# Shifted moving operands, mirrored chunks and merged score products in a tuned encoder block

## The chip, the cores and the metric

The kernel runs on one core of one Trainium2 chip. The metric is the device time of one execution in microseconds. Three runs of the kernel before gave 1113.47, 1114.10 and 1114.87 us; the median is 1114.1 us. TensorE (PE) does the matrix products, VectorE (DVE), ScalarE (ACT) and GpSimd (POOL) the rest, SyncE (SP) issues most of the transfers.

## The reference

One layer of a streaming encoder on 512 positions of 1024 columns: half an FFN, a token mixer, cross attention to 256 memory rows, half an FFN, a final norm. All of it is float32.

```python
x = x + 0.5 * swiglu(rmsnorm(x, ffn1_norm), ffn1_w_gu, ffn1_w_down)
x = x + token_mixing(rmsnorm(x, mix_norm), w_in, lower_bounds, hg_norm, conv_w, conv_norm, w_out)
x = x + cross_attention(rmsnorm(x, xa_norm), rmsnorm(mem, mem_norm), xa_wq, xa_wkv, xa_wo)
x = x + 0.5 * swiglu(rmsnorm(x, ffn2_norm), ffn2_w_gu, ffn2_w_down)
return rmsnorm(x, final_norm)
```

The mixer has four recurrent heads, f = lb + (1 - lb) * sigmoid(fz), k = 1 - f, S_t = diag(f_t) S_{t-1} + k_t v_t^T, o_t = S_t^T silu(q_t), each normed and gated by silu(g), beside a short convolution gb * (3 taps over gc * u) on 512 channels.

## The kernel before

**Products.** An exact product is made of three: each operand is split into a high and a low part of a fast type (`wh`, `wl` for weights, `xh`, `xl` and others for activations), and `product` issues high x high, high x low and low x high. The first operand of a matmul is stationary and is loaded into the array, the second moves through it. ACT makes a unit's high part (`hi`), POOL its low part (`lo`, four instructions of 256 columns); a unit is 1024 columns of weights, and four slots of units rotate. In the FFNs 30 column pairs are computed by seven products of half size (`pair`, `seven`): 256 moving columns each. The other groups move 512.

**Where the operands lie.** Worked out from the allocations, modulo 128 columns of 4 bytes: in the 512-column groups stationary and moving operand both start at column 32; in the 256-column products of the pairs the stationary one starts at 112 and the moving one at 32, as in the two halves of the last group of the second FFN. The 256-column products of the memory's keys (`mh`, `wh`) and of the attention scores (`kTh`, `qhl`) have both at 32. The slots of `wh` and `wl` are read in two ways for this, 48 columns apart (`wh_apart`, `for_256`).

**The mixer.** 28 slots (`MIX_SLOTS`) hold one group of 24 products each, of kind f, q, g (a head's gate, query and output gate), v, B, C or u. After its group, a slot runs the steps of `STEPS` on every engine in the same order. A head starts at slot 0, 7, 12 or 17 and takes nine steps in nine slots: A (log of f, running sum `b` within chunks of 128), L0, L1, L2 (two of the seven levels each, the seventh in L2), K, Q, S, O, N. The decay within a chunk is split into levels of block size 64 to 1: at each level DVE makes the differences of `b` to the block's middle (`differences`, L1250 and L1251), ACT takes their exponential (`decays`), DVE multiplies by q and k (`factors`, L1258 and L1259), PE makes the level's scores (L1740, four matmuls, one for each chunk, of the 64 queries that lie in second halves), and DVE copies them through a mask into `attn` (`take_scores`). PE takes the scores of levels 0 and 1 in step L1, 2 and 3 in L2, 4 and 5 in K, level 6 and the diagonal in Q. Q also transposes the decayed keys, S makes the chunk states, O the output, N the sum of squares for its norm. These small products are float32 and not split; the profile writes two records for each such matmul.

**Order.** Each engine's instructions stand in the order in which the code issues them; semaphores alone join the engines. PE starts a group when the unit's low part is ready and the bank of four groups before has been read (`group_read`).

## Time and profile before

| | us |
|---|---|
| median of three runs | 1114.1 |
| the profiled execution | 1113.43 |
| its span in the trace | 1111.6 |
| PE busy, share of the span | 1100.8, 99% |
| DVE / ACT / POOL busy | 633.8 / 527.4 / 437.1 |
| time in which PE waited for another engine, all rows | 3.8 |

Stages by the trace: first FFN 0 to 357 us (its pairs 72 to 216), mixer 352 to 553, output projection and the memory's keys to 622, cross attention to 757, second FFN to the end (its pairs 802 to 966). The granted clock of PE is 0.998 over the span. A busy PE says little on its own here, since a matmul's record runs on while the next one has started; distances between starts say what one costs.

### The profile page before, as it was taken

The numbers are of one execution on the slowest core, as the hardware profiler recorded it, in microseconds if no ns is written. First come the engines' busy times: TensorE is split into PE (matmuls) and PEld (weight loads), VectorE is DVE, ScalarE is ACT, GpSimd is POOL, SyncE is SP. The second block draws the span as 40 slices with busy tenths as digits, with TensorE's granted clock in tenths as the row PEclk, the third lists the DMA queues.
The fourth block names the chain that finished last, engine by engine and source line by source line (L and its number), as shares of the span: only waits on it lengthen the run. The fifth ranks groups of instructions, "written<-read, shape, count | busy, mean of one in ns | idle before, by whom it ended". The sixth has DMA issues, their size and how long they took to land.

```text
span 1111.6 us, 17495 instructions
## 1 busy us (share of the span) xinstructions
PE 1100.8 (99%) x6434; PEld 972.6 (87%) x6434; DVE 633.8 (57%) x923; ACT 527.4 (47%) x735; POOL 437.1 (39%) x545
## 2 busy tenths in 40 slices
PE   9999999999999999999999999999999999999997
PEld 8889999988888888888888888888899999988886
DVE  7887777442222668888668133466977777440012
ACT  6455555542324555654366443354555555542221
POOL 0000000486665544434548883163000000485651
PEclk9999999999999999999999999999999999999999
DMA  7287675332333221222313442122676675332312
GB/s 241 79 229 184 179 198 170 115 112 97 113 100 108 76 77 57 76 76 77 114 57 127 158 170 76 39 77 76 180 199 180 170 196 170 115 114 96 112 57 76
DMA packets 49458, 136.89 MB, mean 123 GB/s; under 512 B 4736, under 2 KB 11008, under 8 KB 49280
## 3 DMA queue, kind: packets, MB, share of 16 engines
q1 hardware_dynamic: 43888, 118.90, 30.7%
q0 software_dynamic: 4320, 15.73, 8.2%
q10 hardware_dynamic: 1200, 1.57, 0.4%
q8 instruction: 34, 0.56, 0.2%
q14 instruction: 16, 0.13, 0.0%
HBM read 134.09 MB, written 2.10 MB: 123 GB/s over the span
## 4 chain that ended last, share of the span: by engine, by line
PE 53%; POOL 25%; issue 21%; DVE 0%; POOLq 0%; ACT 0%; DVEq 0%
POOL wl L465 25%; PE bank L1497 8%; PE bank L1499 8%; PE bank L1498 8%; PE bank L1606 4%; PE bank L1604 4%; PE bank L1605 4%; PE score L1606 3%; PE score L1604 3%; PE score L1605 3%; PE o_bank L1606 1%; PE o_bank L1605 1%; PE o_bank L1604 1%; PE bank L1561 1%; PE bank L1569 0%
## 5 line engine op out<-in xcount | busy, mean ns | idle before, releaser
L465 POOL TENSOR_TENSOR wl<-raw,wh 128x256 fp32r<-128x256 f32 x511 | 410.9, 837 | 324.7 <-ACT wh L507 281.3
L507 ACT ACTIVATE wh<-raw 128x1024 fp32r<-128x1024 f32 (+1 forms) x120 | 125.6, 1052 | 148.1 <-PE bank L1499 144.0
L1497 PE MATMUL bank<-xh,wh 128*128 128x512 f32 x456 | 182.2, 400 | 0.0
L1499 PE MATMUL bank<-xh,wl 128*128 128x512 f32 x456 | 177.8, 390 | 0.0
L1498 PE MATMUL bank<-xl,wh 128*128 128x512 f32 x456 | 177.7, 390 | 0.0
L479 POOL DMA_DIRECT2D raw<-w_all x30 | 26.1, 868 | 324.8 <-DMA raw<-w_all 324.8
L1497 PE MATMUL bank<-zr,wh 128*128 128x512 f32 (+1 forms) x374 | 140.8, 377 | 0.0
L1499 PE MATMUL bank<-zr,wl 128*128 128x512 f32 (+1 forms) x374 | 140.7, 376 | 0.0
L1498 PE MATMUL bank<-zr,wh 128*128 128x512 f32 (+1 forms) x374 | 140.7, 376 | 0.0
L950 DVE SCALAR_TENSOR_TENSOR x<-bank,x 128x512 f32<-128x512 f32 (+1 forms) x31 | 21.3, 686 | 173.0 <-PE bank L1499 173.0
L1498 PEld LDWEIGHTS bank<-xl,wh 128*128 128x128 f32 x456 | 85.7, 188 | 18.7 <-issue 1.7
L1497 PEld LDWEIGHTS bank<-xh,wh 128*128 128x128 f32 x456 | 85.7, 188 | 18.6 <-issue 1.2
L1499 PEld LDWEIGHTS bank<-xh,wl 128*128 128x128 f32 x456 | 85.6, 188 | 18.2
L520 ACT ACTIVATE wh<-raw 128x1024 fp32r<-128x1024 f32 x50 | 52.8, 1057 | 86.6 <-PE bank L1499 54.7
L1014 DVE TENSOR_TENSOR wl<-raw,wh 128x1024 fp32r<-128x1024 f32 x72 | 87.4, 1216 | 1.4 <-ACT wh L520 0.9
L1498 PEld LDWEIGHTS bank<-zr,wh 128*128 128x128 f32 x374 | 70.3, 188 | 12.9
L1499 PEld LDWEIGHTS bank<-zr,wl 128*128 128x128 f32 x374 | 70.2, 188 | 13.0
L1497 PEld LDWEIGHTS bank<-zr,wh 128*128 128x128 f32 x374 | 70.2, 188 | 12.8
L1497 PE MATMUL bank<-cat_h,wh 128*128 128x512 f32 x128 | 50.6, 395 | 0.5 <-POOL wl L465 0.5
L1498 PE MATMUL bank<-cat_l,wh 128*128 128x512 f32 x128 | 49.9, 389 | 0.0
L1499 PE MATMUL bank<-cat_h,wl 128*128 128x512 f32 x128 | 49.8, 389 | 0.0
L930 DVE TENSOR_TENSOR acc<-acc,sq 128x512 f32<-128x512 f32 x43 | 42.7, 992 | 9.5 <-ACT sq L542 6.6
(304 smaller groups left out, 2586.9 us busy)
## 6 DMA issues: line engine op xcount, KB each, us to landing
raw<-w_all SPq DMA_DIRECT2D x200, 512.0 KB, 3.3
raw<-w_all POOLq DMA_DIRECT2D x30, 512.0 KB, 5.2
zf<-w_all SPq DMA_DIRECT2D x30, 256.0 KB, 4.4
x<-x_t SPq DMA_DIRECT2D x8, 256.0 KB, 6.1
out_t<-x SPq DMA_DIRECT2D x8, 256.0 KB, 2.5
raw<-w_all SPq DMA_DIRECT2D x6, 256.0 KB, 6.1
memf<-mem_t ACTq DMA_DIRECT2D x1, 1024.0 KB, 4.7
raw<-w_all ACTq DMA_DIRECT2D x2, 256.0 KB, 3.9
```

What stands on the lines that cost most here:

```text
L465: ins = nc.gpsimd.tensor_tensor(l[:, slot, two], raw[:, slot, two], h[:, slot, two].bitcast(f32), SUB)
L479: pool.dma_start(raw[:, 2 * p + 1, :], w_all[u, :, :], accum_op=ADD).then_inc(up_added[p], 16)
L507: nc.scalar.activation(unit_hi(u)[:, 0:wide], raw[:, slot, 0:wide], ACT.Copy).then_inc(hi_ready, 1)
L520: nc.scalar.activation(unit_hi(u), raw[:, slot, :], ACT.Copy).then_inc(hi_ready, 1)
L930: V_.tensor_tensor(acc[:, :], acc[:, :], sq[:, n % 2, :], ADD).then_inc(sq_added, 1)
L1014: V_.tensor_tensor(unit_lo(u), raw[:, slot, :], unit_hi(u).bitcast(f32), SUB).then_inc(lo_ready, 1)
L1497: nc.tensor.matmul(out_, a[0], b_[0], start=first, stop=False)
L1498: nc.tensor.matmul(out_, a[0], b_[1], start=False, stop=False)
L1499: return nc.tensor.matmul(out_, a[1], b_[0], start=False, stop=last)
L1604: nc.tensor.matmul(out_, a[0][:, ks], bh, start=first and k == 0, stop=False, skip_group_check=True)
L1605: nc.tensor.matmul(out_, a[0][:, ks], bl, start=False, stop=False, skip_group_check=True)
L1606: last = nc.tensor.matmul(out_, a[1][:, ks], bh, start=False, stop=k == 3, skip_group_check=True)
```

## The change

What the code does differently:

1. The weights have one reading again; in its place `xh` and `xl` get a second one 48 columns further (`xh_apart`), and the other moving operands of the pairs are shifted alike. Modulo 128 columns the stationary operands are all at 32 and the pairs' moving ones at 80. The eight 512-column groups of each FFN that use the normed x (`src=made`) read the shifted copy as well, the last group's halves no longer do.
2. In the mixer every second chunk (0 and 2) is stored mirrored in time, q and f in one tile `qf`. Two chunks then make one 128-wide problem: a level takes two matmuls of 128 queries in place of four of 64. Scores gather in `tri`, and one more masked copy (`triangles`) spreads them over `attn`. Reading and writing q, f and the output takes two instructions of 256 columns where it took one of 512; `factors` is one of 512 where it was two of 256.
3. The masks for this are built on the chip: `make_masks` on DVE ahead of the first FFN's down groups, two matmuls with a mirrored identity (`swap`) ahead of slot 0, two DVE additions after it. Two tiles of V are mirrored by matmuls of 512 columns in float32 (`turn_v`) in slot 6.
4. The difference and exponential of the chunk's end (`kd`) move from K to L2, level 6's difference to L1; ACT runs steps L1 and L2 ahead of a unit's high part; the norm of a head runs a slot later; two heads' convolution taps run a slot later; q2, q3 stand earlier. The product of C and rstd is made once, with rstd squared.

```diff
-             ("B", 0), ("q", 2), ("f", 3), ("g", 1), ("C", 1), ("u", 1),
-             ("q", 3), ("g", 2), ("g", 3), ("B", 1), ("C", 2), ("u", 2), ("B", 2), ("C", 3), ("u", 3), ("B", 3)]
+             ("q", 2), ("B", 0), ("f", 3), ("g", 1), ("q", 3), ("C", 1),
+             ("u", 1), ("g", 2), ("g", 3), ("B", 1), ("C", 2), ("u", 2), ("B", 2), ("C", 3), ("u", 3), ("B", 3)]
...
-                            lhs = X[:, x_slot(l), :]
-                            rhs = lhs.rearrange("p (t n s m) -> p t n s m", t=TT, s=2, m=LEVELS[l])[:, :, :, 1, :]
-                            width = 64
...
-                        for t in range(TT):
-                            last = nc.tensor.matmul(score_bank[s % 2][:, width * t:width * (t + 1)],
-                                                    lhs[:, 128 * t:128 * t + 128], rhs[:, t], start=True, stop=True)
+                        if l < len(LEVELS):
+                            for g in range(2):
+                                last = nc.tensor.matmul(sc[:, 128 * g:128 * g + 128], keys_of(l, g), queries_of(l, g),
+                                                        start=True, stop=True)
...
+        def queries_of(a, g):
+            at_, m = XW * x_slot(a) + 256 * g, LEVELS[a]
+            halves = X[:, at_:at_ + 2 * (256 + m)].rearrange("p (s w) -> p s w", s=2)[:, :, 0:128]
+            return halves.rearrange("p s (n z m) -> p n s z m", z=2, m=m)[:, :, :, 0, :]
...
+            def turn_v(t):
+                if t == 0:
+                    pe.wait_ge(group_read, G_V + TT + 4)
+                else:
+                    pe.wait_ge(v_ready, 1)
+                nc.tensor.matmul(o_bank[:, :], swap.bitcast(f32), V[:, t, :], start=True, stop=True).then_inc(v_turned, 1)
...
+            pe.wait_ge(masks_in, 1)
+            nc.tensor.matmul(score_bank[0][:, :], swap, lower[:, 0:512], start=True, stop=True)
+            nc.tensor.matmul(score_bank[1][:, 0:384], swap, lower[:, 512:896], start=True, stop=True).then_inc(masks_out, 1)
...
-                xx, qq, kk = (blocks(t_, m) for t_ in (X[:, x_slot(a), :], qb[:, h % 2, :], fb[:, h % 2, :]))
-                V_.tensor_tensor(xx[:, :, 1, :], xx[:, :, 1, :], qq[:, :, 1, :], MULT)
-                V_.tensor_tensor(xx[:, :, 0, :], xx[:, :, 0, :], kk[:, :, 0, :], MULT).then_inc(score_in, 1)
+                V_.tensor_tensor(level, level, qk, MULT).then_inc(score_in, 1)
...
+                early = [st for st in STEPS[at] if st[0] == "L" and st[2] > 0]
+                for st in early:
+                    step(*st)
                 ahead(U_MIX + at)
...
-                        act.wait_ge(x_old, (KC - 1) * which + 2 * i + 2)
+                        act.wait_ge(x_old, (KC - 1) * which + 2 * i + 3)
...
-                        group(u0 + P_UNIT, g0 + P_UNIT)
+                        group(u0 + P_UNIT, g0 + P_UNIT, src=made)
```

**PE, slot 6 (the group of f1, then step Q of head 0).** Before:

```order
L1499 MATMUL bank<-xh,wl 128x512
L1740 MATMUL score<-X 128x64 x4
L1740 MATMUL score<-qb,fb 128x128 x4
L1751 MATMUL n_bank<-ident,kd 128x128 x4
L1497 MATMUL bank<-xh,wh 128x512
```

Now, with `qf` for q and f and `both` for the decayed keys:

```order
L1631 MATMUL bank<-xh,wl 128x512
L1857 MATMUL o_bank<-V,ubr 128x512
L1873 MATMUL score<-X 128x128 x2
L1877 MATMUL score<-qf 128x128 x4
L1888 MATMUL n_bank<-ident,both 128x128 x4
L1857 MATMUL o_bank<-V,ubr 128x512
L1629 MATMUL bank<-xh,wh 128x512
```

The level's four matmuls have become two twice as wide, and the two mirroring matmuls stand around the step; their second waits for DVE to have copied out the first.

**DVE, around slots 17 and 18, where head 3 starts.** Before, from the running sum of head 3 to its first differences:

```order
L1285 SCALAR_TENSOR_TENSOR b<-restart,ubuf 128x512
L1389 TENSOR_SCALAR ubuf<-convU,par 128x512
L1390 SCALAR_TENSOR_TENSOR ubuf<-convU,par,ubuf 128x512
L1392 SCALAR_TENSOR_TENSOR ubuf<-convU,par,ubuf 128x512
L1394 TENSOR_TENSOR ubuf<-ubuf,rstd 128x512
L1358 SCALAR_TENSOR_TENSOR qb<-bank,rstd 128x512
L1361 SCALAR_TENSOR_TENSOR qb<-gbuf,qb 128x512
L1328 COPY S<-n_bank 128x128
L1330 SCALAR_TENSOR_TENSOR S<-S,eb,n_bank 128x128 x2
L1250 TENSOR_TENSOR X<-b 128x4x64
```

Now:

```order
L1382 SCALAR_TENSOR_TENSOR b<-restart,lf 128x516
L1502 TENSOR_TENSOR convU<-bank,ubuf 128x512
L1422 COPY S<-n_bank 128x128
L1424 SCALAR_TENSOR_TENSOR S<-S,both,n_bank 128x128 x2
L1345 TENSOR_TENSOR X<-b 128x4x64
L1346 TENSOR_TENSOR X<-b 128x4x64
L1345 TENSOR_TENSOR X<-b 128x8x32
L1346 TENSOR_TENSOR X<-b 128x8x32
L1355 TENSOR_TENSOR X<-X,qf 128x4x2x64
```

The four tap instructions and the two of q no longer stand between the running sum and the differences.

**ACT, slot 14 (f3; step O of head 1, step L1 of head 2).** Before, from the sigmoid of f3 to the exponentials:

```order
L796 ACTIVATE fb<-fb 128x512
L507 ACTIVATE wh<-raw 128x1024
L780 ACTIVATE osq<-o_bank 128x512
L759 ACT_TABLE_LOAD
L759 ACTIVATE X<-X 128x512 x2
```

Now:

```order
L852 ACTIVATE qf<-qf 128x2x2x128
L815 ACT_TABLE_LOAD
L815 ACTIVATE X<-X 128x2x16x16
L815 ACTIVATE X<-X 128x2x32x8
L815 ACTIVATE X<-X 128x2x256
L562 ACTIVATE wh<-raw 128x1024
L838 ACTIVATE osq<-o_bank 128x512
```

The square of the output (`osq`), for which PE's step N waits, now stands behind three exponentials and a unit's high part.

## Rows read from the trace of the kernel before

**Rows 1.** three mixer stretches: us, then each engine's busy us (instructions)
```profile
427.00:457.00 30.00, 29.24 (x159) 24.84 (x158) 25.48 (x44) 17.34 (x22) 13.08 (x16) 1.00 0.16 53
457.00:488.00 31.00, 31.00 (x176) 26.59 (x176) 26.01 (x47) 20.89 (x26) 13.30 (x16) 1.00 0.24 85
488.00:520.00 32.00, 31.04 (x169) 26.23 (x168) 28.12 (x52) 14.63 (x21) 12.31 (x15) 1.00 0.15 51
```

**Rows 2.** PE in order of time: start us, us, what, records
```profile
383.38 1.89 PE L1740 MATMUL score<-X 128*128 128x64 f32 x16
385.08 0.48 PE L1497 MATMUL bank<-wh,xh 128*128 128x512 f32 x1
...
397.95 1.00 PE L1740 MATMUL score<-X 128*128 128x64 f32 x8
398.78 1.11 PE L1740 MATMUL score<-qb,fb 128*128 128x128 f32 x8
399.73 0.60 PE L1751 MATMUL n_bank<-ident,kd 128*128 128x128 f32 x4
...
411.82 1.05 PE L1770 MATMUL o_bank<-attn,V 128*128 128x128 f32 x8
412.71 0.83 PE L1775 MATMUL o_bank<-qb,S 128*128 128x128 f32 x6
```

**Rows 3.** groups of instructions: all the level scores | busy us, mean ns
```profile
L1740 PE MATMUL score<-X 128*128 128x64 f32 x224 | 27.1, 272 | 1.7 <-DVE X L1259 1.7
```

**Rows 4.** PE, a float32 product of 512 columns and its followers
```profile
541.25 1.02 PE L1781 MATMUL n_bank<-osq,ones 128*128 128x512 f32 x2
541.70 0.80 PE L1497 MATMUL bank<-xh,wh 128*128 128x512 f32 x1
542.34 0.40 PE L1498 MATMUL bank<-xl,wh 128*128 128x512 f32 x1
```

**Rows 5.** PE starts 48 records apart: pairs, memory keys, last group
```profile
150.08 0.28 PE L1604 MATMUL score<-xh,wh 128*128 128x256 f32 x1
155.73 0.28 PE L1604 MATMUL score<-zr 128*128 128x256 f32 x1
...
598.53 0.28 PE L1499 MATMUL bank<-mh,wl 128*128 128x256 f32 x1
604.29 0.28 PE L1499 MATMUL bank<-mh,wl 128*128 128x256 f32 x1
...
1087.32 0.28 PE L1499 MATMUL bank<-zr,wl 128*128 128x256 f32 x1
1092.97 0.28 PE L1499 MATMUL bank<-zr,wl 128*128 128x256 f32 x1
```

**Rows 6.** DVE, start of the mixer [idle before, releaser]
```profile
360.05 0.69 DVE L1356 TENSOR_TENSOR fb<-bank,rstd 128x512 f32<-128x512 f32 x1 [1.44 <-issue]
...
368.43 0.68 DVE L1358 SCALAR_TENSOR_TENSOR qb<-bank,rstd 128x512 f32<-128x512 f32 x1
```

**Rows 7.** PE at the bank that q0 leaves
```profile
368.70 0.39 PE L1499 MATMUL bank<-wh,xl 128*128 128x512 f32 x1
369.17 0.50 PE L1497 MATMUL bank<-wh,xh 128*128 128x512 f32 x1
```

**Rows 8.** DVE, the factors of one level, slow and fast
```profile
417.64 0.95 DVE L1259 TENSOR_TENSOR X<-X,fb 128x256 f32<-128x256 f32 x1
418.52 0.41 DVE L1258 TENSOR_TENSOR X<-X,qb 128x256 f32<-128x256 f32 x1
```

**Rows 9.** PE where it waited for DVE, heads 1 and 3
```profile
435.20 2.00 PE L1740 MATMUL score<-X 128*128 128x64 f32 x16 [0.76 <-DVE X L1259]
...
497.44 2.00 PE L1740 MATMUL score<-X 128*128 128x64 f32 x16 [0.96 <-DVE X L1259]
```

**Rows 10.** ACT, slot 14
```profile
459.58 1.06 ACT L507 ACTIVATE wh<-raw 128x1024 fp32r<-128x1024 f32 x1
460.54 0.58 ACT L780 ACTIVATE osq<-o_bank 128x512 f32<-128x512 f32 x1
```

More of the change, by code:

```diff
@@ L99 @@
     _s.sort(key=lambda st: st[0] == "N")
+NORMED = [[h for kind, h, _ in (STEPS[at - 1] if at else []) if kind == "N"] for at in range(len(MIX_SLOTS))]
 def block_kernel(nc, w_all, x_t, mem_t, params, consts_mask, ident_d, out):
@@ L461, in _, with lo @@
         def _(pool):
-            def lo(slot, h=wh, l=wl, pieces=KC):
-                for k in range(0, pieces, 2):
+            def lo(slot):
+                for k in range(0, KC, 2):
                     two = slice(128 * k, 128 * k + 256)
-                    ins = nc.gpsimd.tensor_tensor(l[:, slot, two], raw[:, slot, two], h[:, slot, two].bitcast(f32), SUB)
+                    ins = nc.gpsimd.tensor_tensor(wl[:, slot, two], raw[:, slot, two], wh[:, slot, two].bitcast(f32), SUB)
                 ins.then_inc(lo_ready, 1)
@@ L488, in _ @@
             pairs(U_FFN2, 1)
-            whole(U_FFN2 + P_UNIT, NU - SLOTS)
-            for u in range(NU - SLOTS, NU):
-                pool.wait_ge(hi_ready, u + 1)
-                if for_256(u):
-                    lo(u % SLOTS, wh_apart, wl_apart)
-                else:
-                    lo(u % SLOTS, pieces=DOWN_SPLIT[-1])
+            whole(U_FFN2 + P_UNIT, NU)
         @block.scalar
@@ L503, in hi @@
                 act.wait_ge(raw_loaded[slot], u // SLOTS * 16)
-                nearer = for_256(u + 1 - SLOTS) and not for_256(u)
-                wide = 128 * DOWN_SPLIT[-1] if u == NU - SLOTS else UNIT
-                act.wait_ge(unit_used, u + 1 - SLOTS + nearer)
-                nc.scalar.activation(unit_hi(u)[:, 0:wide], raw[:, slot, 0:wide], ACT.Copy).then_inc(hi_ready, 1)
+                act.wait_ge(unit_used, u + 1 - SLOTS)
+                nc.scalar.activation(wh[:, slot, :], raw[:, slot, :], ACT.Copy).then_inc(hi_ready, 1)
             def ahead(u):
@@ new lines, in silu @@
+            def silu(kind, c):
+                dve.wait_ge(act_out, FN[kind, c] + 1)
+                if kind == "g":
+                    dst = gb[:, c % 2, :]
+                    V_.scalar_tensor_tensor(out=dst, in0=half_tanh, scalar=1.0, in1=dst, op0=ADD, op1=MULT)\
+                        .then_inc(silu_done, 1)
+                else:
+                    for p in range(2):
+                        dst = q_of(c)[:, :, p, :]
+                        last = V_.scalar_tensor_tensor(out=dst, in0=by_chunk(half_tanh)[:, :, p, :], scalar=1.0,
+                                                       in1=dst, op0=ADD, op1=MULT)
+                    last.then_inc(silu_done, 1)
@@ new lines, in taps @@
+            def taps(at, c):
+                dve.wait_ge(group_read, SLOT_GROUP[at] + 5)
+                w = [pcol("convw", CC * k + c) for k in range(3)]
+                link(V_.tensor_scalar(convV, convU[:, 2:], w[2], None, MULT))
+                link(V_.scalar_tensor_tensor(out=convV, in0=convU[:, 1:1 + T], scalar=w[1],
+                                             in1=convV, op0=MULT, op1=ADD))
+                link(V_.scalar_tensor_tensor(out=convV, in0=convU[:, 0:T], scalar=w[0],
+                                             in1=convV, op0=MULT, op1=ADD))
+                link(V_.tensor_tensor(convV, convV, rstd[:, :], MULT))
@@ L1595, in ffn @@
                     group(u0 + c, g0 + c, release=x_old if c == 2 * old - 1 else None)
+                made = xh_apart, xl_apart
                 for c in range(2 * old, 2 * pre):
-                    group(u0 + c, g0 + c, ready=(xn_lo, KC * which) if c == 2 * old else None)
+                    group(u0 + c, g0 + c, src=made, ready=(xn_lo, KC * which) if c == 2 * old else None)
                 def seven(out_, a, at, b_, cols_, first):
@@ L1659, in ffn @@
                 for c in range(P_UNIT + 1, N_UP):
-                    group(u0 + c, g0 + c)
+                    group(u0 + c, g0 + c, src=made)
                 ud, gd, nd = u0 + N_UP, g0 + N_UP, len(DOWN_SPLIT)
@@ L1694, in ffn @@
                         for k in range(n):
[L1695 removed]
+                            last = product(bank[(gd + KC - 1 + h) % 4][:, HALVES[h]], wpair(u % SLOTS, 128 * k, 128 * k + 128),
                                            (hid(j)[0][:, HALVES[h]], hid(j)[1][:, HALVES[h]]), j == 0, j == FC - 1)
```

389 lines of the change are left out of this document (245 added, 144 removed).

## The prediction

> **What bounds the kernel now.** I read the busy shares first, then the waits of PE, then PE in order of time. PE is busy for 99% of the span at full clock, and all its waits for other engines come to 3.8 us (both in the table above), of which 1.7 lie in the mixer, at two places [rows 9]. So the time is the sum of the distances between PE's starts, and an edit counts by what it does to that sum or by a wait that it brings. PE cannot run ahead of DVE, though: in the mixer DVE is busy for 25.5 of 30, 26.0 of 31 and 28.1 of 32 us [rows 1], 86% of the stretch. No other stage of the change has an engine that close behind PE.
>
> **Scores of the levels, removed and added.** Before, 224 records of 64 columns [rows 3] stand in what would be 14 blocks of 16. One block takes 385.08 - 383.38 = 1.70 us [rows 2], so 14 take 23.8 us. A matmul is two records: 0.213 us. Now there are 56 matmuls of 128 columns. Rows show two of this size: the attention's 8 records in 0.89 us, 0.111 each, and the diagonal's 8 records in 0.95 us, 0.119 each [rows 2]. I take the middle, 0.115: 112 records are 12.9 us. The term is -10.9 us, with -11.4 and -10.5 as near ends. That a matmul of twice the columns costs nearly the same is the heart of the forecast. What the rows cannot show is the new reading pattern: two runs of queries, at level 1 every second element. At 64 columns the same stride cost nothing (level 6's block of 8 records took 0.83 us [rows 2], half a block and no more), but the stream was then shorter than what bounds the product, and now it is about as long. A float32 product of 512 columns takes 542.34 - 541.25 less 0.23 for the split product between, 0.86 us [rows 4], so a stream of 128 is worth 0.215 us; doubled it would be 0.43. For level 1 alone that is 8 x 0.2 = 1.6 us, for all seven 11 us. I take none of it, since the strides at 64 columns cost nothing, and keep both ends.
>
> The Trainium skill speaks against the gain. Its page "TensorE: Matmul & The Clock Gate", section "Back-to-back issue gap", gives the distance of two matmuls as columns over 2.4 GHz and a small constant, while its section on LDWEIGHTS gives a load as 128 columns over 1.2 GHz, whatever is streamed. By the first the 28 x 64 and 14 x 128 columns of a head cost the same and the term is near zero; by the second it is near a half. The trace agrees with the second: 0.106 and 0.111 us for a record of 64 and of 128 columns [rows 2].
>
> **Mirrored V, added.** Two float32 matmuls of 512 columns on PE's path, 0.86 us each [rows 4]: +1.7 us. The second waits until DVE has copied the first out, about 0.7 us for an instruction of 512 columns from PSUM [rows 6]. Between them stand level 6 (2 matmuls), the diagonal (4) and four transposes, over 1.5 us, so I cost that wait at nothing; without the cover it would be 0.7. DVE has no work due then.
>
> **Masks, added.** The two matmuls ahead of slot 0 move 896 columns of the split type; at 0.118 us for 256 [rows 5] that is +0.4 us. `make_masks`, some 25 DVE instructions of at most 0.7 us, stands ahead of the down groups, where each group gives PE 15 us of work (66 products at the 0.23 us of a split product of 512 columns) and DVE 3 instructions; it is hidden. At the mixer's start DVE gets two additions from PSUM, a memset and rstd squared ahead of f0: 0.69 + 0.5 + 0.3 + 0.7 = 2.2 us (0.69 for 512 columns from PSUM [rows 6], the smaller ones by their columns). DVE sat idle for 1.44 us there [rows 6], so f0 comes 0.8 us later, and with it the running sum of head 0 and the reading of q0 behind it. PE already waits for q0's bank: 369.17 - 368.70 is 0.47 where 0.23 is usual [rows 7]. PE itself comes 0.4 later, so this wait grows by 0.4 us: +0.4. The scores of levels 0 and 1 come after it and gain from the shorter `factors`; no wait there.
>
> **Waits in the mixer.** The two old ones go, -1.7 us [rows 9]. Head 1's came from the norm and the product of C ahead of the differences, head 3's from four taps and q3; all four pieces are moved or gone, as the order shows. Two new kinds are possible. First, slot 19 now holds g2, step L1 of head 3 and the taps: 0.7 + 4 differences + 2 copies + 2 factors of 512 + the two differences of level 6 + 0.7 + 2.7 us. With 0.34 us between the fast instructions of 256 columns this is 8.4 us, and about 10 when POOL works beside it (0.95 against 0.41 us for one instruction [rows 8]). PE's work from that slot to the next is 5.4 us for its group (24 products of 0.227), 1.6 for step Q and 0.9 for step S or K, 7.9 us. DVE starts slot 20 some 2 us late, needs 4 to 6 us to the factors of level 5, and PE needs them 6.9 us after its own group: a wait of about 1 us. Second, ACT's square of the output in slots 14 and 19 now stands behind the exponential of level 6, for which DVE must have done that slot's factors, and a unit's high part: DVE 4.9 to 8.6 us, then 0.6 + 1.06 + 0.58 [rows 10] gives 7.2 to 10.9 us after the group, against 8.8 us until PE's step N. Half a microsecond each, twice. Together +2.0 us; the ends are 0 and 5.
>
> The units' high parts also stand behind L1 and L2 on ACT, and POOL's low parts and PE's group behind them. They are made three slots, about 20 us, before PE needs them; a delay of 9 us is hidden. DVE's extra copy (0.7 us a head) is paid by the product of C that is gone (0.7), the split reads (0.07 each) by the merged factors.
>
> **The shift of the operands.** The distance between stationary and moving operand, modulo 128 columns, is 112 - 32 = 80 in the pairs before and 32 - 80 = -48, again 80, now. The pairs run at 5.65 / 48 = 117.7 ns, and the keys of the memory, distance 0, at 5.76 / 48 = 120.0 ns [rows 5]. Same distance, same cost: the term of 2520 products is 0. Sixteen groups of 512 columns, 384 products, go from distance 0 to 80. No row has 512 columns at 80; by the 2.3 ns of the 256-column rows that is -0.9 us, by the same in the other direction +0.9. I take -0.4, half of the nearest row. The last group's 132 products go from 80 (117.7 ns, rows 5) to 0: +0.3 us. ACT's split of the normed x waits for one more of PE's k steps, 0.7 us, in a stretch where the result is ready more than 1 us early: nothing.
>
> **Sum.** -10.9 + 1.7 + 0.4 + 0.4 - 1.7 + 2.0 - 0.4 + 0.3 = -8.2 us. The profiled execution took 1113.4 us, its span 1111.6, the rest start and end that stay; 1113.4 - 8.2 = 1105.2. It lies 0.7 below the median of the runs, so I forecast 1105.9 us.
>
> **Rivals.**
> 1. DVE becomes the bound of the mixer. For: the 86% of rows 1, and PE's share of a head shrinks by 2.7 us while DVE's work does not. Against: 93 us with 79.6 busy become 86.4 us, so DVE would be at 92%, under 1. If the contention of rows 8 strikes more of the merged 512-column instructions, waits of 7 us rather than 2: 1111. The skill's page "SBUF — State Buffer", section "Who interferes with whom", says that a DVE instruction with two SBUF inputs and a GpSimd instruction that reads SBUF lock each other out entirely; the two times of one instruction in the trace agree with that. It gives no time of its own here.
> 2. The distance counts with its sign, not modulo 128. Then the pairs move by the 2.3 ns of rows 5 or more: 2520 x 2.3 = 5.8 us. Dearer: 1111.7. Cheaper: 1100.1. For: nothing in the trace has a distance of -48. Against: over the pairs the distance of whole multiples of 128 varies from product to product and the 117.7 does not.
> 3. It gets slower: the scores cost by columns, or, which comes to the same, the broken stream of the new queries counts double. Place: the 56 level matmuls, 0.43 us in place of 0.23. Price: +11 us, so the gain of 10.9 is gone and the additions stay, 1117. It decides from 0.38 us a matmul upward. For: no row has a broken stream at 128 columns. Against: strides at 64 columns cost nothing, and rows 2 has 0.111 us at 128.
>
> **From this to the numbers.** The sum as worked out: 73%, with 1103.0 to 1109.5 as its own range (waits from 0 to 5, near ends of the scores, 0.9 either way for the 512-column groups). DVE the bound: 12%. Pairs dearer 5%, cheaper 6%. Slower by the stream: 4%. The range that leaves out 2 in 10 at most is 1101.5 to 1110.5. A change of 0.2%, 2.2 us, is about what a measurement of this kernel tells from none. Faster: all of the first, 9 of the 12, 3 of the 5 and the 6: 91%. Within 0.2%: 5%. Slower: 4%.
>
> **What the profile would show.** Right: 112 level records of 128 columns at 0.11 to 0.12 us from start to start; two float32 products `V,ubr` of 0.86 us each in slot 6; pairs still at 117.7 ns; PE's waits in the mixer under 4 us, at step K of head 3 or at step N; the mixer 8 to 9 us shorter and all other stages alike within 1 us. Wrong: level records above 0.19 us (rival 3), PE waiting on `X` or `osq` for over 6 us in all (rival 1), or the stretch of the pairs changed by more than 1 us in each FFN (rival 2).

## The result, and the profile after

Four runs of the changed kernel gave 1100.7 to 1101.28 us, median 1100.88, against 1113.84 for the kernel before (four runs). The ratio is 0.9883, 95% interval 0.9866 to 0.9900. The forecast was 1105.9, with a range of 1101.5 to 1110.5: the right sign, but 8.2 us expected and 13 found, just outside the range. The profiled execution has a span of 1098.9 us, 12.7 less than before, and PE is again busy for 99% of it.

The starts of PE give the lengths of the stages, and where the 12.7 us lie:

| stretch | before, us | after, us | difference |
|---|---|---|---|
| to the first pairs | 72.0 | 72.5 | +0.5 |
| pairs of the first FFN | 144.0 | 138.9 | -5.1 |
| down groups, masks | 142.6 | 143.5 | +0.9 |
| mixer | 183.7 | 177.6 | -6.1 |
| start of the output projection | 15.9 | 17.2 | +1.3 |
| to the second FFN | 205.1 | 205.1 | 0 |
| its groups ahead of the pairs | 38.6 | 39.2 | +0.6 |
| its pairs | 163.8 | 158.0 | -5.8 |
| its down groups | 121.0 | 121.5 | +0.5 |
| last group and end | 24.9 | 25.4 | +0.5 |

The forecast had all its gain in the mixer and none in the pairs. In fact the pairs bring 10.9 us and the mixer, with the stretch behind it, 4.8; the other stretches lose 3.0. PE in order of time in the changed kernel (start us, us, what), 48 products apart as in [rows 5]: first in the pairs, then in the last group.

```profile
150.07 0.28 PE L1734 MATMUL score<-xh,wh 128*128 128x256 f32 x1
155.51 0.28 PE L1734 MATMUL score<-zr,wh 128*128 128x256 f32 x1
...
1074.11 0.28 PE L1631 MATMUL bank<-zr,wl 128*128 128x256 f32 x1
1079.87 0.28 PE L1631 MATMUL bank<-zr,wl 128*128 128x256 f32 x1
```

A pair's product now takes 5.44 / 48 = 113.3 ns where it took 117.7, and 2520 of them make 11 us. The last group's products went to 5.76 / 48 = 120.0 ns as forecast.

The scores of two levels, and of the last level with the mirroring products around it, in the changed kernel:

```profile
372.85 1.05 PE L1873 MATMUL score<-X 128*128 128x128 f32 x8
373.65 0.48 PE L1629 MATMUL bank<-wh,xh 128*128 128x512 f32 x1
...
392.77 1.02 PE L1857 MATMUL o_bank<-V,ubr 128*128 128x512 f32 x2
393.63 0.82 PE L1873 MATMUL score<-X 128*128 128x128 f32 x4
394.28 1.06 PE L1877 MATMUL score<-qf 128*128 128x128 f32 x8
```

Four matmuls of 128 columns take 0.80 us from their start to the next product's, 0.100 per record. [rows 2] had 1.70 for the eight of 64 columns that did the same work, 0.106 per record. The last level's two take 0.65, so 0.163 per record: this one reading is dearer. Over all blocks, from start to start and without waits, the levels went from 24.3 to 13.3 us.

PE's waits for other engines, the mixer's and those near it (total us, times, longest):

```profile
PE n_bank L1897 <- DVE kdT L1414: 3.2, 3, 1.6
...
PE n_bank L1672 <- DVE acc L993: 1.0, 1, 1.0
PE n_bank L1919 <- ACT osq L838: 1.0, 1, 1.0
PE bank L1629 <- DVE qf L1487: 0.6, 1, 0.6
...
PE bank L1629 <- DVE V L1509: 0.5, 1, 0.5
```

The two waits of [rows 9] are gone, but step S now waits three times for DVE's copy of the transposed decayed keys, `kdT`. The longest is in head 1 (PE, then DVE ahead of it; in brackets the idle time and its releaser):

```profile
437.02 0.47 PE L1629 MATMUL bank<-xh,wh 128*128 128x512 f32 x1
...
444.34 0.91 PE L1897 MATMUL n_bank<-V,kdT 128*128 128x128 f32 x6 [1.59 <-DVE kdT L1414]
```

```profile
435.83 0.47 DVE L1463 TENSOR_SCALAR ubuf<-convU,par 128x512 f32<-128x512 f32 x1
436.34 1.10 DVE L1464 SCALAR_TENSOR_TENSOR ubuf<-convU,par,ubuf 128x512 f32<-128x512 f32 x1
437.48 1.11 DVE L1466 SCALAR_TENSOR_TENSOR ubuf<-convU,par,ubuf 128x512 f32<-128x512 f32 x1
438.62 1.11 DVE L1468 TENSOR_TENSOR ubuf<-ubuf,rstd 128x512 f32<-128x512 f32 x1
...
442.38 1.21 DVE L1412 TENSOR_TENSOR qf<-qf,both 128x512 f32<-128x512 f32 x1
443.51 0.68 DVE L1414 COPY kdT<-n_bank 128x512 f32<-128x512 f32 x1
```

Ahead of the copy stand the taps, which the change put there (L1463 to L1468), and then the scores and q times decay. In head 3 (1.43 us at 518.16) it is the norm of head 2, a slot later now, during which DVE is idle for 2.9 us.

### The profile page after: what moved, and what is told of

Same layout as the page of the kernel before. It is cut to its first block, busy times and chain, and to the rows that moved or that the text cites. A ratio compares the mean times of both kernels' runs of the same rounds, so it can differ in the third digit from the quotient of the medians.

```text
span 1098.9 us, 17317 instructions
## 1 busy us (share of the span) xinstructions
PE 1083.4 (99%) x6328; PEld 951.3 (87%) x6328; DVE 638.4 (58%) x944; ACT 525.8 (48%) x738; POOL 441.0 (40%) x546
## 4 chain that ended last, share of the span: by engine, by line
PE 52%; POOL 25%; issue 21%; DVE 1%; POOLq 0%; DMA 0%; ACT 0%; DVEq 0%; SPq 0%; ACTq 0%
POOL wl L528 25%; PE bank L1629 8%; PE bank L1631 8%; PE bank L1630 8%; PE bank L1734 4%; PE bank L1735 4%; PE bank L1736 4%; PE score L1734 3%; PE score L1735 3%; PE score L1736 3%; PE o_bank L1734 1%; PE o_bank L1735 1%; PE o_bank L1736 1%; PE bank L1690 1%; PE bank L1694 0%
## 5 line engine op out<-in xcount | busy, mean ns | idle before, releaser
L562 ACT ACTIVATE wh<-raw 128x1024 fp32r<-128x1024 f32 x120 | 125.7, 1053 | 137.7 <-PE bank L1631 135.6
L575 ACT ACTIVATE wh<-raw 128x1024 fp32r<-128x1024 f32 x50 | 52.8, 1056 | 86.7 <-PE bank L1631 54.0
L1631 PEld LDWEIGHTS bank<-zr,wl 128*128 128x128 f32 x374 | 70.4, 188 | 12.7
```

Source lines behind the costliest of these rows:

```text
L562: nc.scalar.activation(wh[:, slot, :], raw[:, slot, :], ACT.Copy).then_inc(hi_ready, 1)
L575: nc.scalar.activation(wh[:, slot, :], raw[:, slot, :], ACT.Copy).then_inc(hi_ready, 1)
L1631: return nc.tensor.matmul(out_, a[1], b_[0], start=False, stop=last)
```

## The experiments

In the studies of stretches alone, (w, m) are the columns at which the stationary and the moving operand start, counted from a multiple of 128. Distance is m - w modulo 128, so the pairs of both kernels have 48, which the prediction counts the other way round as 80; distance 80 below is another one. A stretch's pace is the time from its start to the next thing's start, over its products; where a float32 product stands ahead or behind, this is 1 to 7 ns too much, and paces of such stretches are read from the products in their midst. Each study is one run, at a granted clock of 0.996 or 0.997.

### 1. Which place of the operands costs what

> No encoder here: only stretches of 72 split-type products, stationary operand starting at column w, moving operand at column m (modulo 128 below), first all stretches one after the other, then all again with a float32 product of 512 columns ahead of each. The other engines are idle meanwhile. Known from the two kernels, for 256 columns: (32,32) 120.0 ns a product, (112,32) 117.8 in the kernel before, (32,80) 113.3 in the changed one; for 512 columns (32,32) 226.7 and (32,80) about 230. Theory A, the prediction's: only the distance modulo 128 counts. Then (32,80), (112,32), (80,128), (0,48), (64,112) and (112,160), all at distance 48 modulo 128, give one and the same number here, and what differed in the kernels came from something else (the traffic of other engines, or what stood ahead). Theory B: the place of one operand by itself counts. Then (112,32) gives 117.8 and (32,80) 113.3 again, and of the others those with the moving operand at 32 or the stationary one at 112 go with the first. Theory C: the distance counts with a longer period. Then (32,208) and (112,160) differ from (32,80) by more than 2 ns. For the 256-column stretches at other distances A expects one smooth curve between 113 and 120 ns, the largest at 0 and 128.

Edit: a kernel of its own, 49 lines of this kind (bank, w, m, columns; 72 products, high x high, high x low and low x high in turn).

```python
stretch(1, 32, 80, 256, lambda *a, **k: nc.tensor.matmul(*a, **k))
```

The first eight, (32,32), (32,48), (32,64), (32,80), (32,96), (32,112), (32,128) and (32,144), of which five are shown:

```profile
37.59 8.79 PE L55 MATMUL bank<-data 128*128 128x256 f32 x72
46.22 8.64 PE L56 MATMUL bank<-data 128*128 128x256 f32 x72
54.71 8.70 PE L57 MATMUL bank<-data 128*128 128x256 f32 x72
63.25 8.35 PE L58 MATMUL bank<-data 128*128 128x256 f32 x72
71.44 8.78 PE L59 MATMUL bank<-data 128*128 128x256 f32 x72
```

From start to start: 8.63, 8.49, 8.54 and 8.19 us, so 119.9, 117.9, 118.6 and 113.7 ns for distances 0, 16, 32 and 48. (112,32) ran at 117.8 and (32,80) at 113.7, as in the two kernels. That would be theory B, but in the second pass, behind a float32 product, (112,32), (112,160), (80,128) and (32,208) ran at 113.3, all of which had 117.8 in the first; (64,112) went the other way, from 113.3 to 117.8, and (160,80) stayed at 117.8. One place of the operands had two paces. No theory of place alone, A, B or C, can say that. For 512 columns: 227.2 at distance 0, 233.3 at 48, 229.0 at 80, alike within 0.5 ns in both passes.

### 2. What decides between the two paces

> No encoder here: 24 split products of 512 columns, then one thing or nothing, then 60 products of 256 columns, 28 times over. The 60 are at (112,32) (stationary and moving start modulo 128, as in the kernel before) or at (32,80) (as in the changed one), the distance 48 both times. Between stand: nothing, a wait of PE for another engine, a float32 product of 128, 64 or 512 columns, or a split product of 128 or 256 columns at the place of the 512-column ones. Theory D, from the first study: at distance 48 there are two paces, 113.5 and 117.8 ns a product, each kept once it is taken, and what stands ahead of a stretch decides which. Then (112,32) straight after 512 columns at (32,32), the kernel before, runs at 117.8, and (32,80) straight after 512 columns at (32,80), the changed kernel, at 113.4; behind a float32 product of 512 columns both run at 113.6, and at least one other thing in between changes the pace of the former. Theory B, that the place of an operand decides: (112,32) has one pace in all its fourteen stretches, (32,80) one in all of its own.

Edit: `stretch` of 24 x 512 columns, one thing, `stretch` of 60 x 256. In the trace of these stretches, (112,32) behind 512 columns at (32,32), first directly, then with one split product of 256 columns between, then (112,32) behind 512 columns at (112,32):

```profile
27.30 7.23 PE L68 MATMUL bank<-data 128*128 128x256 f32 x60
34.37 5.64 PE L69 MATMUL bank<-data 128*128 128x512 f32 x24
...
91.63 6.96 PE L83 MATMUL bank<-data 128*128 128x256 f32 x60
98.43 5.64 PE L84 MATMUL bank<-data 128*128 128x512 f32 x24
...
117.17 6.97 PE L88 MATMUL bank<-data 128*128 128x256 f32 x60
123.97 1.32 PE L89 MATMUL bank<-data 128*128 128x512 f32 x5
```

7.07 us for 60 is 117.8 ns, 6.80 is 113.3. Nothing about the 60 products differs between the first and the second. (32,80) straight behind (32,80) took 6.81, straight behind (32,32) 7.06. In all, 8 of the 14 stretches at (112,32) and 9 of the 14 at (32,80) were fast. That is theory D, and B falls. One part of D's expectation missed: behind a float32 product of 512 columns only (112,32) with 512 columns at (32,32) ahead was fast, and the other three were at 117.8. Only the wait (behind a float32 product of 128 columns) was followed by the fast pace at all four places, and in experiment 10 not even that. No rule for which entry is fast comes out of this; it was found by trying.

### 3. The kernel before with one product more

> The kernel before, with one split product of 256 columns put between the last 512-column group and the pairs of each FFN (stationary and moving operand both at column 32 modulo 128, its result overwritten). Nothing else is changed, no operand is moved. Theory D, that the pace of the pairs is set by what stands ahead of them: they go from 117.8 to 113.4 ns, 2520 products by 4.4 ns, so 11 us less than before, about 1102.8 us. Theory B, that the place of the operands sets it: the pairs stay at 117.8 and the time at 1113.8 plus 0.2.

```diff
+                pe.wait_ge(lo_ready, u0 + 2 * pre + 1)
+                nc.tensor.matmul(E_bank[0], wh[:, 0, 0:128], xh[:, 0, left], start=True, stop=True)
                 first_product(0, n0, 0)
```

1102.86 us (1102.62 to 1102.98), ratio 0.9899, interval 0.9883 to 0.9916. PE, 48 products of the pairs, at the same time as in [rows 5]:

```profile
150.04 0.28 PE L1606 MATMUL score<-xh,wl 128*128 128x256 f32 x1
155.48 0.28 PE L1606 MATMUL score<-zr,wl 128*128 128x256 f32 x1
```

113.3 ns, through the 1164 and 1332 products ahead of the 512-column group in the last pair, with every operand where it was. The added wait is the one that `first_product` makes in any case, so the product itself is what differs. One product ahead of each FFN's pairs is worth 10.9 us. This is the decisive run: the shift of the operands is not needed for the gain of the pairs, and the rest of the change is worth 1102.9 - 1100.9 = 2.0 us.

### 4. The changed kernel, pushed into the slow pace

> The changed kernel, with one float32 product of 512 columns put ahead of the pairs of each FFN, the one thing that brought (32,80) behind 512 columns at (32,80) to the slow pace in the second study. Theory D: the pairs go from 113.3 to 117.8 ns, 11 us, and the two products cost up to 0.9 us each: about 1113 us, the whole gain of the change gone. Theory B: 1100.9 plus 0.9 to 1.7, about 1102.2.

```diff
+                nc.tensor.matmul(score_bank[0][:, :], ones[:, :], acc[:, :], start=True, stop=True)
                 first_product(0, n0, 0)
```

1115.2 us (1113.5 to 1116.6), ratio 1.0011, interval 1.0002 to 1.0021.

```profile
150.05 0.28 PE L1735 MATMUL bank<-xl,zr 128*128 128x256 f32 x1
155.70 0.28 PE L1735 MATMUL score<-xl,wh 128*128 128x256 f32 x1
```

117.7 ns. Both kernels can have either pace, and what stands ahead of the pairs chooses. The median is 2.2 us above the expectation. Five of the ten runs lie at 1113.5 to 1114.4 us, with a granted clock of 0.998 or 0.999 over the span, and five at 1116.0 to 1116.6 with 0.997. The profiled one, 1114.4, is of the first kind, with 3.8 us of waits at step S where the changed kernel had 3.2. What the second kind loses no trace of this run shows; experiment 6 has a trace of such a run.

### 5. The copy of kdT first

> The changed kernel, with DVE's copy of the transposed keys (kdT) ahead of the diagonal's scores, the spreading of the triangles and q times decay in step Q, where it stood behind them. In the trace of the changed kernel PE waits for this copy three times at step S, 3.2 us in all (1.59, 0.17, 1.43). What is put behind it is 0.74 + 0.74 + 1.2 us. Theory: the waits are nothing but this queue on DVE, so they go, and the time falls by 2.5 to 3.2 us to about 1098. Rival: DVE is the bound of these stretches, so that the same microseconds come back as waits at step O or at the next bank, and the time stays within 0.7 us of 1100.9.

```diff
                     take_scores(h, 6)
-                    take_scores(h, 7)
-                    V_.tensor_tensor(q_of(h), q_of(h), eb, MULT).then_inc(qd_ready, 1)
                     dve.wait_ge(n_done, N["Q", h] + 1)
                     V_.tensor_copy(kdT[:, :, :], n_bank[:, :].rearrange("p (t k) -> p t k", t=TT))\
                         .then_inc(kdT_ready, 1)
+                    take_scores(h, 7)
+                    V_.tensor_tensor(q_of(h), q_of(h), eb, MULT).then_inc(qd_ready, 1)
```

1099.27 us (1099.18 to 1099.55), 1.6 below the changed kernel, ratio to before 0.9868, interval 0.9852 to 0.9885. This is the fastest version of all, though 1.6 us is less than the 2.5 to 3.2 of the theory. PE's waits:

```profile
PE o_bank L1908 <- DVE S L1424: 1.4, 1, 1.4
...
PE score L1873 <- DVE X L1355: 0.6, 1, 0.6
```

The 3.2 us at step S are gone; 2.0 came back within the next slot, at step O of head 1 (1.4) and step L1 of head 2 (0.6). Half of each view was right: in heads 2 and 3 the queue was all, behind head 1 the microseconds came back as other waits for DVE.

### 6. No shift at all

> The changed kernel with the operands' shift taken out: the normed x and the other moving operands of the pairs at column 32 modulo 128 like the stationary ones, distance 0 in every product. The first studies give one pace for distance 0 with 256 columns, 119.9 ns, and 227 for 512 columns against 233.3 at distance 48. Theory: the 2520 products of the pairs cost 6.6 ns more each, +16.7 us, the 384 of 512 columns 6.3 ns less, -2.4 us: 1115.2 us, slower than the kernel before although the mixer is shorter. The prediction's view, by which a distance's cost is small (2.3 ns): 1100.9 plus 5.8 minus 0.4, 1106.3.

```diff
-        xh_apart, xl_apart = at_column(xh_both, APART), at_column(xl_both, APART)
+        xh_apart, xl_apart = xh, xl
...
-            at = first * T + EVEN + APART - 128
+            at = first * T + EVEN
```

1117.75 us (1115.2 to 1117.85), ratio 1.0027, interval 1.0017 to 1.0037.

```profile
150.02 0.28 PE L1736 MATMUL bank<-zr,wl 128*128 128x256 f32 x1
155.78 0.28 PE L1736 MATMUL o_bank<-zr,wl 128*128 128x256 f32 x1
```

120.0 ns, and 226.8 for 512 columns. The theory's 1115.2 is the lowest of the runs: four lie at 1115.2 to 1116.5 us, with a granted clock of 0.998 or 0.999 over the span, and five at 1117.8 with 0.996 or 0.997. The profiled one is of the second kind. Its waits at step S are 5.3 us instead of 3.2, and behind the first of them, 2.14 us long, the clock that PE was granted fell to half, the 1.2 GHz level (the third figure from the end of the row; ahead of it stand the busy times of the five rows of engines):

```profile
451.60:455.00 3.40, 3.40 (x11) 3.01 (x12) 2.63 (x3) 2.38 (x4) 2.13 (x4) 0.50 0.28 83
```

In it, split products of 512 columns start 0.43 us apart instead of 0.23. Half of 3.4 us is 1.7 us of lost work (an estimate). In the profiled run of experiment 4 PE waited 2.16 us at the same place and the clock stayed, so waits alike in length were followed by either. Against no shift the shift brings 17 us, 14 to 16 where the mean clock was 0.998 or 0.999. Against the kernel before, which had a shift too, it brings 11, because only its entry was bad.

### 7. The taps back in their slot

> The changed kernel with the convolution taps of the first channel block back in their own slot on DVE (slot 10, behind step L2 of head 1) instead of slot 11 (behind step K). Theory: the wait of 1.59 us at step S of head 1 comes from these four instructions, 4.1 us on DVE between step K and step Q, so it shrinks to under 0.5 us, and the time to about 1099.6. Rival: in their old place they delay step K or the reading of the next bank by as much, a wait of 1 to 2 us appears there, and the time is 1100.9 within 0.7.

```diff
-                if kind == "u" and MIX_SLOTS[at + 1] == ("B", c):
+                if kind == "u" and (MIX_SLOTS[at + 1] == ("B", c) or c == 0):
...
-                if at and MIX_SLOTS[at - 1][0] == "u" and kind != "B":
+                if at and MIX_SLOTS[at - 1][0] == "u" and kind != "B" and MIX_SLOTS[at - 1][1] > 0:
```

1104.73 us (1104.31 to 1104.85): 3.8 slower than the changed kernel.

```profile
PE score L1873 <- DVE tri L1365: 3.3, 1, 3.3
PE n_bank L1897 <- DVE kdT L1414: 3.2, 2, 1.7
```

The theory had the cause right and the consequence wrong. Head 1's wait for `kdT` is gone (448.02, no wait), but step Q waits 3.25 us for the reading of a score bank, which is now behind the same four instructions, and head 2's wait grew from 0.17 to 1.72. Behind the wait of 3.25 us the granted clock fell to half here too, and all four runs have a mean of 0.996 over the span:

```profile
439.70:443.10 3.40, 3.40 (x16) 3.21 (x15) 2.77 (x7) 2.96 (x4) 2.91 (x4) 0.50 0.02 5
```

The waits at steps Q, S and N grew by 2.2 us in all, and half of 3.4 us is 1.7 (an estimate), together about the 3.8. So the rival's mechanism holds, with a longer wait than its 1 to 2 us and the clock on top, and its time of 1100.9 does not: the later taps of the change are right.

### 8. The root of head 2 first

> The kernel with kdT copied first (1099.3 us), and besides on ACT the inverse root of head 2's norm ahead of the exponentials of step L2 of head 3 in slot 20. In the trace DVE stands idle for 2.2 and 0.7 us at 507 to 511 waiting for that root, behind which step Q of head 3 is queued. Theory: that idle time goes, but the wait of PE that hung on it went already with the copy moved, so the time stays at 1099.3 within 0.5. Rival: the remaining waits of PE in the mixer shrink too, 1098.5 or less. A third way: the exponentials come later and PE waits for step K's factors, 1 to 2 us more.

```diff
-                early = [st for st in STEPS[at] if st[0] == "L" and st[2] > 0]
+                early = [st for st in STEPS[at] if st == ("N", 2, 0)] + [st for st in STEPS[at] if st[0] == "L" and st[2] > 0]
```

1100.38 us (1100.01 to 1100.67), 1.1 above experiment 5, whose edit this kernel has too. The third way came, though smaller: PE's waits for the factors `X` rose from 0.6 to 1.2 us, the new one at step K of head 3. DVE's 2.2 us of idle time are gone and 1.1 stand at 503.06 instead, where it waits for the exponentials; nothing was gained by filling the former.

### 9. What a float32 product's reading costs

> No encoder here. 40 float32 products of 128 stationary columns for each of 24 readings of the moving operand: 128, 64, 256, 512 columns in one run; 64 and 128 columns in blocks of m with m skipped between them, m from 64 to 1; and the reading of the changed kernel's levels, blocks of m from two chunks in turn. Theory, from the changed kernel's trace (0.21 us for a level's product of 128 columns, but 0.325 for the last level's): a float32 product costs 0.21 us for 64 and for 128 columns alike, so doubling the columns is free, and blocks of 2 and more cost nothing extra, while m = 1 at 128 columns costs 0.1 us more. Rival: the last level's 0.325 comes from what stands behind it, and m = 1 costs 0.21 like the rest.

The readings of the changed kernel's levels with m = 64, 4, 2 and 1, 40 products (80 records) each, then 256 columns in one run:

```profile
191.33 9.09 PE L80 MATMUL bank<-x 128*128 128x128 f32 x80
...
227.06 9.10 PE L84 MATMUL bank<-x 128*128 128x128 f32 x80
235.99 9.77 PE L85 MATMUL bank<-x 128*128 128x128 f32 x80
245.60 13.49 PE L86 MATMUL bank<-x 128*128 128x128 f32 x80
258.92 17.44 PE L87 MATMUL bank<-x 128*128 128x256 f32 x80
```

From start to start a record takes 111.7 ns at m = 64, 32, 16 and 8, the same for 128 and for 64 columns in one run (111.6 and 111.0), 111.6 at m = 4, 120.1 at m = 2, 166.5 at m = 1, and 215.9 for 256 columns. Every second element of a single run of 256 costs only 113.4. So doubling the columns from 64 to 128 is free; blocks of 2 cost 8 ns, against the theory's nothing, and single elements in turn cost half as much again, as it said. The last level's eight matmuls lose 16 x 55 ns = 0.9 us to it.

### 10. Other distances, alone and in the kernel

> No encoder here. 60 products of 256 columns with the stationary operand at column 32 and the moving one d columns further, for d = 0, 8, 16, 24, 32, 40, 44, 48, 52, 56 and 60, three times each: behind 24 products of 512 columns at distance 0, behind 24 at distance d, and behind these with one split product of 256 columns at distance 0 in between. Theory D: at 48 the first gives 117.8 ns, the second 113.4; near 48 there are two paces too, and at 0 one, 120, whatever stands ahead. Rival: the two paces belong to the one distance 48 alone, and every other has a single one between 113 and 120.

(32,48) straight behind 512 columns at (32,32), then straight behind 512 at (32,48):

```profile
103.41 7.23 PE L78 MATMUL bank<-data 128*128 128x256 f32 x60
110.48 5.67 PE L79 MATMUL bank<-data 128*128 128x512 f32 x24
115.99 6.96 PE L80 MATMUL bank<-data 128*128 128x256 f32 x60
122.79 5.66 PE L81 MATMUL bank<-data 128*128 128x512 f32 x24
```

Distance 16 has the same two paces, 117.8 and 113.3. Distance 0 has one, 120, and 24, 44, 56 and 60 have one each, between 117 and 120. At 8, 32 and 40 two lie 1.1 to 1.4 ns apart, and at 52 two, 119.2 and 116.7. None is under 113.3, so neither theory was quite right. The 512-column stretches had one pace at most distances, but at 52 two, 230.0 and 234.4 ns, and at 60 two, 233.3 and 236.7.

> The kernel with kdT copied first (1099.3 us), and the shifted moving operands 48 columns ahead of the plain ones instead of 48 behind: modulo 128 they start at 112 with the stationary ones at 32, distance 80, which is 16 modulo 64. The stretches alone gave the same numbers for distances 64 columns apart (16 and 80: 117.8 both, 48 and 112... the same 113.7), and at 16, behind 512 columns at 16, the fast pace of 113.3; 512 columns at 16 or 80 took 229.0 ns against 233.3 at 48. Theory: the pairs keep 113.3 ns, the 384 products of 512 columns with the shifted operand gain 4.3 ns each, 1.6 us: 1097.7 us. Rival: at 80 the pairs fall into the slow pace behind their entry, 2520 by 4.4 ns: 1108.7.

```diff
-        xh, xl = at_column(xh_both, 0), at_column(xl_both, 0)
-        xh_apart, xl_apart = at_column(xh_both, APART), at_column(xl_both, APART)
+        xh, xl = at_column(xh_both, APART), at_column(xl_both, APART)
+        xh_apart, xl_apart = at_column(xh_both, 0), at_column(xl_both, 0)
...
-            at = first * T + EVEN + APART - 128
+            at = first * T + EVEN - APART
```

1108.82 us (1108.78 to 1109.35): the rival, at its price. The kernel also has the edit of experiment 5, and some small tiles changed places.

```profile
150.11 0.28 PE L1735 MATMUL bank<-zr,wh 128*128 128x256 f32 x1
155.76 0.28 PE L1735 MATMUL o_bank<-zr,wh 128*128 128x256 f32 x1
```

> No encoder here: 24 split products of 512 columns, one thing or nothing, 60 products of 256 columns, all with the stationary operand at 32 and the moving one at 112 (distance 80), 48 (distance 16) or 80 (distance 48), with ten things in between: nothing, split products of 128, 256 or 384 columns, two of them, float32 products of 64, 128 and 512 columns, a wait. Theory D: distance 80 has the two paces too, 117.8 and 113.4 ns; behind 512 columns at 80 it takes the slow one, as in the kernel with distance 80, and at least one of the things puts it into the fast one. Rival: distance 80 has only the slow pace, whatever stands ahead, and only distance 16 and 48 have two.

At (32,112) all ten entries left the slow pace (117.8 ns in the midst of each stretch): the rival. At (32,48) it was 113.3 straight behind 512 columns and 117.8 with a split product of 256 columns at distance 0 between; with one at distance 16, or a float32 product of 64 or 128 columns, it stayed 113.3. At (32,80) straight behind 512 at (32,80) it was 117.7, where experiment 2 had 113.3: the 24 products ahead are not the whole history.

> The kernel with kdT copied first (1099.3 us) and every shifted moving operand 16 columns from the plain ones in place of 48, so that the distance to the stationary ones is 16 in the pairs and in the 384 products of 512 columns ahead and behind. Stretches alone at (32,48), straight behind 512 columns at (32,48), ran at 113.3 ns twice, at (32,112) at 117.8 always; 512 columns at distance 16 took 229.0 ns against 233.3 at 48. Theory D, paces set by distance and entry together: the pairs keep 113.3 ns and the 384 products gain 4.3 ns each: 1097.7 us. Rival: the entry in the kernel leaves the slow pace at 16, 2520 by 4.4 ns more: 1108.8.

```diff
-APART = 48
-EVEN = 96
-HID_AT = HID * T + EVEN
+APART = 16
+EVEN = 32
+HID_AT = HID * T + EVEN + 128
...
-            at = first * T + EVEN + APART - 128
+            at = first * T + EVEN + APART
```

1109.28 us (1108.75 to 1109.76), pairs at 117.8: what the stretches alone showed at 16 did not carry over. This kernel and the next three have the edit of experiment 5 too. Then three entries for it, the line of experiment 3 with `xh` (plain), with `xh_apart` (shifted), and a float32 product of 128 columns:

> The kernel with distance 16 (1109.3 us, its pairs at the slow pace), with the entry that brought the kernel before to the fast one: a split product of 256 columns with both operands at 32, ahead of the pairs of each FFN. Theory D: the entry decides, and one of the three entries tried here gives 113.3 ns and about 1098 us. The stretches alone gave the slow pace at 16 behind this product, so this one may be not the one: 1109.5. Rival: distance 16 has only the slow pace in the kernel, whatever the entry.

> The same kernel, the entry a split product of 256 columns at distance 16. The stretches alone kept their pace behind this product, so I expect the slow one here, 1109.5 us; fast would be 1098.

> The same kernel, the entry a float32 product of 128 columns. The stretches alone ran at the fast pace behind it at distance 16: 1098 us; with the rival 1109.5.

1108.79, 1108.53 and 1109.07 us, pairs at 117.8 in all three. The expectation for the float32 entry, 1098, failed, and so did theory D's, that one of the three would be fast. Yet the twelve products behind the 512-column group inside the last pair took 1.25 us for eleven (113.6 ns each) with the shifted and the float32 entry, and 1.29 or 1.30 (117.3 and 118.2) with the plain one and with none. So distance 16 has its fast pace in the kernel too. The entry stands 1164 products of 256 columns, all slow, and 24 of 512 ahead of these twelve and still decides; no entry that puts the pairs into the fast pace was found.

## Why the prediction was wrong

- **What bounds the kernel.** Right. PE's starts add up to the span, and what the change gained and lost is found in them.
- **Scores of the levels.** Right: -11.0 against the -10.9 of the sum, in part by luck. The old blocks took 24.3 us and not 23.8. A new matmul took mostly 0.20 us and not 0.23 in six levels, but 0.33 in the last, whose reading costs 0.9 us in all; the prediction took strides to be free because they are at 64 columns. The Trainium skill's rule for loads ("TensorE: Matmul & The Clock Gate", LDWEIGHTS) against its rule of the issue gap was decided by experiment 9 for the first: 111 ns for 64 and for 128 columns.
- **Mirrored V, masks, q0's bank.** V costs 1.7 us as in [rows 4]. From start to start q0's bank takes 1.01 us where it took 0.47, so +0.5 against the forecast 0.4. The new wait of 0.5 us for the bank that V's copy holds was not in it.
- **Waits in the mixer.** Mis-sized: 2.0 was taken, 4.7 came besides q0's (`kdT` 3.2, `osq` 1.0, V 0.5). ACT's square was named (1.0 us, once, not twice). The other wait was put at step K of head 3, behind the factors; it came at step S. The working followed DVE only as far as the factors and let step Q out, where the moved taps and the moved norm stand in the same queue. The 4.7 us lie between the sum's 2 and rival 1's 7. In the same way 1.0 us came behind the mixer, where head 3's later norm stands ahead of the last taps and the sum of their squares; the forecast did not look there. That the cause is the norm is read from the order on DVE (DVE starts it at 538.57, 7.2 us behind PE's products for it, and before the change at 545.26, 4.0 behind them) and was not tried.
- **Shift of the operands.** This is the step that failed: "Same distance, same cost: the term of 2520 products is 0." The distance was right and unchanged, and the cost was not a function of it. The rows of [rows 5] held one pace of two. What the runs showed in its place: at this one distance a product takes 113.3 or 117.8 ns, and what stands ahead of the pairs decides which, 10.9 us for two products (experiments 3 and 4). The hint was in the trace of before: with the same operands, the last group ran at 117.7 ns ([rows 5]) up to the norm's products in its midst and at 113.5 behind them, 46 products from the first row to the second here:

```profile
1097.61 0.28 PE L1498 MATMUL bank<-zr,wh 128*128 128x256 f32 x1
...
1102.83 0.28 PE L1499 MATMUL bank<-zr,wl 128*128 128x256 f32 x1
```

The prediction makes no use of it. Its own sign for rival 2, a stretch of the pairs changed by more than 1 us, came true. Rival 2's cheaper side named almost this number, 1100.1, for a reason that is wrong: the sign of the distance plays no part, since the kernel before reaches 113.3 with its own (experiment 3).
- **512 columns at the new distance.** Wrong in sign: 233.3 ns at 48 and 227.2 at 0, so +6 ns for each of 384 products, +2.4 us, where the prediction took -0.4 by analogy to 256 columns.
- **Last group.** +0.3 forecast; 120.0 ns as said, but it also lost its fast second half, so +0.5.

The sum with what was measured: -11.0 + 1.7 + 0.4 + 0.5 - 1.7 + 4.7 + 1.0 + 2.4 + 0.5 - 10.9 = -12.4 us, against 12.7 of the spans. The mixer's waits and the 512-column groups were taken 6.5 us too cheap and the pairs 10.9 too dear, so that the forecast lies only 5 us off is luck.

## What to carry to other kernels

Where a trace shows long runs of one form of product, compare their pace before and behind an interruption: two values with the same operands mean that the better pace may be had by what stands ahead, here 11 us for two products whose result nobody reads; which product does it has to be tried, and at distance 16 none of three did. When an instruction is moved to another place on a busy engine, follow that engine's queue through every later step for which the bound engine waits, not only the next. And a move that helps one wait may be paid at a neighbouring one, so try a copy's place before a stage's.

## What the hardware showed unexpectedly

- Products of 256 columns at distance 48 run at 113.3 or 117.8 ns each and keep their pace for over 1300 products. A single product ahead of them switches it, and at distance 16 its effect showed behind 1164 slow products. What is remembered between them, and why distance 80 showed the slow pace alone, stays open.
- Products of 512 columns took 227.2 ns at distance 0, 229.0 at 16 and 80 and 233.3 at 48 in every stretch; at 52 and 60 they too have two paces. Of the distances measured, 0 is the best for 512 columns and, with 120 ns, among the worst for 256.
- A float32 product's record takes 111.7 ns with blocks of 4 or more taken in turn from two chunks, 120.1 with blocks of 2 and 166.5 with single elements, though every second element of one run costs 113.4.
- A wait of PE can be paid twice. Behind waits of 2.14 and 3.25 us the granted clock was half, from 451.6 to 455.0 us in experiment 6 and from 439.7 to 443.1 in experiment 7; behind one of 2.16 us in experiment 4 it was not. In experiments 4 and 6 the runs with a mean clock of 0.996 or 0.997 are the longer ones, by some 2 us.
